# Token chunk outermost in the plain product units of a four-layer decoder trunk

## The reference, cut to what matters

```python
for i in range(DEPTH):                       # DEPTH = 4
    kind, j = i % N_MIXERS, i // N_MIXERS    # a, b, c, a
    hp = rms_norm(xp, norm_pre[i])           # prompt, 1024 tokens x 1024
    hs = rms_norm(xs, norm_pre[i])           # samples, 8 tokens x 1024
    # mixer: h @ w_in -> mixing, gates -> (...) @ w_out
    xp = xp + rms_norm(yp, norm_post[i])
    xs = xs + rms_norm(ys, norm_post[i])

# mixer_a:  u, v, g = split(h @ w_in)        w_in 1024 x 6144
#           out = (gelu(u) * mixed(v) * silu(g)) @ w_out     w_out 2048 x 1024
# mixer_b:  z = h @ w_in (q, k, v, gate)     w_in 1024 x 2304, w_out 1024 x 1024
# mixer_c:  xr, g = split(h @ w_in)          w_in 1024 x 2048, w_out 1024 x 1024
```

## Time and profile before

| | us |
|---|---|
| median of 3 runs | 2337.61 (2337.34 to 2337.77) |
| the profiled execution, its own time | 2337.06 |
| its span, first to last instruction | 2334.9 |
| PE busy | 2297.7, 98% of the span, 15487 matmuls |
| PEld busy | 2216.9, 15487 loads |
| DVE busy | 1227.9, 53% |
| ACT busy | 898.2, 38% |
| POOL busy | 127.5, 5% |

### The profile page before, as it was taken

The page is one execution under the profiler, slowest core; times in us unless marked ns, Lnnn a source line. Parts: engine busy times, 40 slices in busy tenths (PEclk is TensorE's granted clock), DMA queues, the critical chain, the costliest instruction groups (busy, mean ns, idle before and its releaser), DMA issues.

```text
span 2334.9 us, 36097 instructions
## 1 busy us (share of the span) xinstructions
PE 2297.7 (98%) x15487; PEld 2216.9 (95%) x15487; DVE 1227.9 (53%) x1708; ACT 898.2 (38%) x1295; POOL 127.5 (5%) x109
## 2 busy tenths in 40 slices
PE   8999999999999999999999999999999999999997
PEld 7999999999999898887999999989999999999997
DVE  4444445445423747667367878275444544545235
ACT  6223322323322525556362475363224233233232
POOL 0000000000000004344000110000000000000000
PEclk9999999999999999999999999999999999999999
DMA  4111111111121341111322111331111111111213
GB/s 140 46 46 46 46 44 39 46 38 45 46 92 46 112 141 46 56 46 37 109 85 81 46 46 40 118 116 58 46 46 46 37 46 46 37 46 46 91 47 109
DMA packets 58654, 145.86 MB, mean 62 GB/s; under 512 B 8936, under 2 KB 29560, under 8 KB 58488
## 3 DMA queue, kind: packets, MB, share of 16 engines
q1 hardware_dynamic: 55088, 138.66, 18.5%
q10 hardware_dynamic: 3408, 4.90, 0.8%
HBM read 121.47 MB, written 18.37 MB: 60 GB/s over the span
## 4 chain that ended last, share of the span: by engine, by line
PE 88%; DVE 6%; DVEq 2%; ACT 1%; DMA 1%; issue 1%; ACTq 0%; SPq 0%
PE ps L583 63%; PE ps L609 8%; PE ps L839 5%; PE ps L669 3%; PE ps L751 2%; PE ps L857 1%; PE ps L885 1%; PE ps L896 1%; PE ps L744 1%; DVE l_hs L2090 1%; PE ps L683 1%; DVE l_sc L1910 1%; DVE w_lo L1482 1%; PE ps L871 1%; ACTq L1426 0%
## 5 line engine op out<-in xcount | busy, mean ns | idle before, releaser
L583 PE MATMUL ps<-l_h_hi,w_hi 128*128 128x344 f32 x2448 | 789.1, 322 | 2.9 <-DVE w_lo L1482 2.9
L583 PE MATMUL ps<-l_h_hi,w_lo 128*128 128x344 f32 x2448 | 780.1, 319 | 0.0
L583 PE MATMUL ps<-l_h_lo,w_hi 128*128 128x344 f32 x2448 | 779.8, 319 | 0.0
L583 PEld LDWEIGHTS ps<-l_h_hi,w_hi 128*128 128x128 f32 x2448 | 459.5, 188 | 6.8 <-DVE w_lo L1482 4.1
L583 PEld LDWEIGHTS ps<-l_h_hi,w_lo 128*128 128x128 f32 x2448 | 459.6, 188 | 0.6
L583 PEld LDWEIGHTS ps<-l_h_lo,w_hi 128*128 128x128 f32 x2448 | 459.4, 188 | 0.0
L1482 DVE TENSOR_TENSOR w_lo<-w_raw,w_hi 128x1024 fp32r<-128x1024 f32 x181 | 225.2, 1244 | 238.1 <-ACT w_hi L1029 227.9
L583 PE MATMUL ps<-l_y_lo,w_hi 128*128 128x344 f32 x816 | 260.1, 319 | 0.0
L583 PE MATMUL ps<-l_y_hi,w_hi 128*128 128x344 f32 x726 | 232.6, 320 | 0.9 <-DVEq L2104 0.8
L583 PE MATMUL ps<-l_y_hi,w_lo 128*128 128x344 f32 x726 | 231.4, 319 | 0.0
L1645 DVE TENSOR_TENSOR l_tmp<-ps,rx 128x1032 f32<-128x1032 f32 x64 | 78.8, 1232 | 281.2 <-PE ps L583 281.0
(11 more groups left out here) (260 smaller groups left out, 3645.7 us busy)
## 6 DMA issues: line engine op xcount, KB each, us to landing
w_raw<-in_wu SPq DMA_DIRECT2D x181, 512.0 KB, 3.5
x_save<-x SPq DMA_DIRECT2D x9, 1376.0 KB, 7.0
x<-x_save SPq DMA_DIRECT2D x21, 516.0 KB, 7.1
out_y<-x SPq DMA_DIRECT2D x5, 688.0 KB, 3.5
l_sw<-l_q SPq DMA_DIRECT2D x24, 129.0 KB, 3.4
x<-in_xt SPq DMA_DIRECT2D x4, 688.0 KB, 9.6
x<-in_xt SPq DMA_DIRECT2D x5, 516.0 KB, 7.1
x<-in_xt ACTq DMA_DIRECT2D x3, 516.0 KB, 3.7
```

The lines of the kernel that those rows point to most:

```text
L583: mm = nc.tensor.matmul(ps[:, 3 * slot + ch, 0:CW], wt[:, w, k, :], mv[:, k, ch * CW:(ch + 1) * CW], start=(k == 0 and t == 0), stop=(k == ...
```

## The change

`product` gets an inner function `parts(k, ch)` with the three matmuls of one k and one chunk. Where `ready`, `free` and `between` are all absent, the chunk becomes the outer loop and k the inner one: 24 matmuls in a row add into one bank, then come 24 for the next. In the other units the loops stay as they were. The number of instructions, their operands, the start and stop flags of each bank, the waits ahead of a unit and the signal after it don't change.

```diff
             def product(slot, w, hi, lo, ready=None, free=None, between=None):
 
+                def parts(k, ch):
+                    for t, (wt, mv) in enumerate(((w_hi, hi), (w_lo, hi), (w_hi, lo))):
+                        mm = nc.tensor.matmul(ps[:, 3 * slot + ch, 0:CW], wt[:, w, k, :], mv[:, k, ch * CW:(ch + 1) * CW],
+                                              start=(k == 0 and t == 0), stop=(k == KT - 1 and t == 2))
+                    return mm
+
+                if ready is None and free is None and between is None:
+                    for ch in range(CH):
+                        for k in range(KT):
+                            mm = parts(k, ch)
+                    return mm
                 for k in range(KT):
                     if ready is not None:
 
                         pe.wait_ge(*ready(k))
                     for ch in range(CH):
-                        for t, (wt, mv) in enumerate(((w_hi, hi), (w_lo, hi), (w_hi, lo))):
-                            mm = nc.tensor.matmul(ps[:, 3 * slot + ch, 0:CW], wt[:, w, k, :],
-                                                  mv[:, k, ch * CW:(ch + 1) * CW],
-                                                  start=(k == 0 and t == 0), stop=(k == KT - 1 and t == 2))
+                        mm = parts(k, ch)
                     if free is not None:
                         mm.then_inc(free, 1)
```

## The result

The changed kernel takes 2342.95 us (median of 11 runs, 2341.44 to 2344.00), the kernel before 2337.61 (11 runs): a ratio of 1.0023, 95% interval 1.0015 to 1.0032. That is 5.3 us slower, with an interval from 3.5 to 7.5.

A forecast was written before the change was run, and what follows sets the result against it. PE bounds the kernel through plain matmuls' number times start-to-start distance. 98 x 0.054 = 5.3 us plus 26 x 0.033 = 0.9 us makes 6.2 us more: 2343.8 us against 2337.61, 8-in-10 range 2336.9 to 2346.9.

The forecast's parts named there:

- The bound: Plain units of `product` on PE: not fed late; they cost matmul count times start-to-start distance, 156.66 ns.
- The units touched: Plain units of `product`: 98 with `h` and 26 with `y`, 124 units with 8928 matmuls.
- The price of an `h` unit: Plain units moving `h`: 0.054 us more each, read from one-bank chunks in L609.
- The price of a `y` unit: Plain units moving `y`: 0.033 us more each, read from one-bank chunks in the trace.
- The sum: All plain units on PE's path: 5.3 us for `h` plus 0.9 for `y`, 6.2 us more.
- Rival 1: One-bank chunks' excess comes from signals or partial-product order and disappears: 2337.6 us; chance 0.43 with all sums under 4.7 us.
- Rival 2: Each third distance of L583: bank changes cost up to 40 ns, so removing 2604 gives 2233 us; chance 0.05.
- Rival 3: Plain units slower by more, 0.07 us per `h` unit: 8.2 us, up to 11, so 2345.8 us; chance 0.12.
- The rule: Matmul pace: skill page gives 145.8 ns against 156.66; if bank changes explained it, 85 us won, 2252 us.

The follow-up runs named there:

- e1: Changed kernel's walk through weights and moving tiles, but the bank changes every three matmuls as in the kernel before; 2342.95 us, ratio 1.0027.
- e8: Against the changed kernel: k outermost, then partial product, then chunk, so bank and moving address change at every matmul; 2346.25 us, one run.
- e4: Weights and banks in the order of the kernel before; only the moving operand walks k inner, chunk outer; 2343.28 us, one run.
- e11: Kernel before, but layer 0's first 12 plain units try six partial-product orders, six units per walk (before's, the change's); 2337.35 us, one run.
- e2: Walk of the kernel before, but 24 matmuls in a row into one bank as in the changed kernel; 2337.08 us, ratio 1.0002.
- e9: Kernel before, but each of layer 0's first 12 plain units moves only one chunk, at its own start offset; 2338.22 us, one run.
- e3: Moving tiles and banks in the order of the kernel before; only the weight tile steps every three matmuls as in the change; 2338.84 us, one run.
- e12: Changed kernel with k = (3 i + 5 chunk) mod 8, unbroken steps of 96 modulo 256 bytes; ten last-layer units walk otherwise; 2339.20 us, ratio 1.0007.
- e10: Kernel before, but layer 0's first 10 plain units walk the 24 moving places in other steps, the last two as the change; 2338.26 us, one run.

## Why the prediction was right, point by point

- *The bound.* Right: the plain units' pace carried the change. PE's waits and the other engines stayed as they were.
- *The units touched.* Right: e1 to e8 give the plain branch of `product` a line of its own, and the trace has 8928 matmuls on it, as counted.
- *The price of an `h` unit.* 0.054 us was read from L609's one-bank chunks; the changed unit is 11.333 against 11.28, 0.053 more. L609 was the right model because with `h` it walks the moving operand in the same order, k by k and chunk after chunk, and e4 shows that this walk is what costs. Its wait and signal for each chunk and its order of partial products, which the prediction left open, are without effect (e11 for the order; for the signal, the agreement of the two numbers).
- *The price of a `y` unit.* 0.033 was read from the earlier trace rows. In layer b 216 matmuls went from 33.84 to 34.00: 0.053 for each of its three units, the same as for `h` and more than forecast. The rows were a wrong model here. `last_triple` doesn't run the chunks of a unit one after another: its order in the code (`TRIPLE`) begins with chunk 0 of each of its three units. So the three chunks from 751.30 to 762.61 are chunk 0 three times, and not one of each number as in the changed unit.
- *The sum.* 6.2 us forecast, 5.3 measured with an interval of 3.5 to 7.5. In the profiled executions the plain units are 5.6 us longer, and errors of both signs make the difference from 6.2, so part of the closeness is luck. The `y` units were put too low, by 0.4 us. A layer a took 2.44 us for 52 units, 0.047 each: where other matmuls stand between units, the chain's pieces of 11.28, 11.48 and 11.51 us became 11.32, 11.53 and 11.53, which is 0.04 a unit on the mean and not 0.054. And of the 8 plain units in the middle of layer c that the prediction said might be absorbed, 6 were: there the chain runs through DVE, and two units with what stands between them took 36.02 us from start to start (1350.30 to 1386.32) before and 36.02 (1354.51 to 1390.53) after. The prediction had left their 0.3 us in. The profiled execution was 6.9 us longer in span, and the 1.3 us beyond the plain units' 5.6 lie in the first loads and the attention; one execution doesn't tell such differences from scatter.
- *Rival 1, nothing happens.* Its reason, that the excess belonged to L609's signals or partial products, fell with e11 and with e1, which has neither. The measured 0.23%, with an interval from 0.15 to 0.32, is nevertheless so close to the 0.2% at which this case and the forecast part that the time alone wouldn't tell them apart; the paces do.
- *Rival 2, a change of bank costs time.* Out by e2: with 3 changes of bank in place of 24 a unit keeps 33.84 us for 216 matmuls. The price of a bank change is below 0.01 us / 63 = 0.2 ns (three units, 21 changes each).
- *Rival 3, as the model.* Its 0.02 us in a chunk was nearly right for chunk 0, but the three chunks differ: in the changed unit they begin at 62.34, 66.11 and 69.89 us, and the next unit at 73.67. So three times chunk 0 is too much, 0.07 against 0.053. Its range of 0.02 to 0.11 for three chunks was also wider than the rounding of the starts allows: 0.005 us in each of the two makes it 0.04 to 0.10.
- *The rule.* The section "Back-to-back issue gap" of the Trainium skill's page "TensorE: Matmul & The Clock Gate" gives the formula of which the prediction made 145.8 ns, an estimate. The prediction left out that the same section gives it for an isolated matmul, and for a stream of weight loads and matmuls gives measured figures instead, 81 ns for 128 columns and 131 ns for 512. The traces here agree with neither: 156.66 ns for 344 columns. Over the offsets of e9 the pace goes from 155.0 to 160.0 ns at the same granted clock of 1.00; the formula has no term for the start offset, and none of the orders comes near it.

What the prediction didn't have is the cause. It forecast by analogy with chunks already in the trace and said that it didn't know what made their excess. It named the memory walk, but neither which operand (e3, e4) nor that the offset modulo 256 bytes counts (e9).

## What to carry to other kernels

Before reordering a product loop, look whether the kernel already has a loop with the new order, and compare the starts of whole chunks, not the lengths of single matmuls (319 to 323 ns in both kernels). Check also that those chunks follow one another as in the new loop, which the `y` rows here didn't. A reorder that keeps every instruction can still cost 0.5% of a matmul's pace through the addresses at which the moving operand begins. Where the order has to change, it may pay to keep the sequence of start offsets: e12 has the chunk outermost and the old pace.

## What the runs showed of the hardware that was not expected

- The pace of this kernel's matmuls (344 columns, float32r, a weight load each) depends on the start of the moving stream modulo 256 bytes: 11.16 us for 72 at an offset of 64 (from the tile's start), 11.52 at 160.
- It also depends on what went before: an even run of steps of 96 modulo 256, with three matmuls at each place, gives 156.67 ns where the mean of the eight offsets alone is 157.4; the same steps at every matmul give 158.1 (11.38 us for 72, e12); after a break the first 24 matmuls cost up to 0.03 us more (unit 5 of e10). Why the order counts isn't settled. Nor is whether all streams begun at the best offset, 64, would run at 155.0 ns in complete products: that needs other tile sizes and chunk borders, and wasn't tried. By e9 it would be worth 0.12 us a unit, an estimate.
- The bank that a matmul adds into (e1, e2), the order in which the weight tiles are taken (e3) and the order of the three partial products at one place (e11) had no effect that the profile can show.
